# A hybrid encoder step with routed experts on one core: the order in which an expert's rows are laid over the 96 places of its block

## The chip, the cores and the metric

The kernel runs on one core of one Trainium2 chip. The metric is the device time of one execution in microseconds. The kernel before took 1379.6 us (median of three runs, 1379.13 to 1380.07).

## What is computed

One layer of a streaming encoder over 576 tokens (512 of a prompt, 64 of a sample), model width 1024. A first part (an input projection, a causal pooling mixer, gated linear attention, an output projection, a layer norm) gives `h`. Then comes a mixture of 32 experts, of which each token takes 4, and a second layer norm:

```python
def _moe(x2, w_router, b_router, w_gu, b_gu, w_down, b_down):
    logits = jnp.dot(x2, w_router) + b_router
    top_val, top_idx = lax.top_k(logits, TOP_K)          # 4 of 32
    gates = jax.nn.softmax(top_val, axis=-1)
    ...
    def block_fn(args):
        e, rows = args
        xb = x2[rows]
        gu = jnp.dot(xb, w_gu[e]) + b_gu[e]              # 1024 -> 2048
        gate, up = gu[:, :EXPERT_FF], gu[:, EXPERT_FF:]
        gate = jnp.minimum(gate, SWIGLU_LIMIT)
        up = jnp.clip(up, -SWIGLU_LIMIT, SWIGLU_LIMIT)
        hmid = gate * jax.nn.sigmoid(SWIGLU_ALPHA * gate) * (up + 1.0)
        return jnp.dot(hmid, w_down[e]) + b_down[e]      # 1024 -> 1024
    ...
    y = jax.ops.segment_sum(y_rows * sorted_gate[:, None], sorted_tok, num_segments=N)
```

576 tokens times 4 experts are 2304 rows, 72 for a mean expert. With the reference's own inputs its router gives the 32 experts 73, 75, 72, 70, 77, 61, 85, 76, 74, 61, 63, 82, 69, 75, 79, 75, 87, 65, 78, 69, 59, 52, 54, 92, 77, 71, 84, 73, 63, 80, 67 and 66 rows.

## The kernel before

All weights are float32 in HBM. An expert has four pieces of `w_gu` and two of `w_down`, 2 MB each. SyncE loads them (L423 to L441, `load` at L432) into a ring of eight slots, each piece 128 partitions of 16 KB, in the order of use. A piece is issued when the slot it goes to has been read: by VectorE's splits (`split_done`) for a slot that held `w_gu`, by TensorE's down product (`down_read`) for one that held `w_down`.

ScalarE turns each quarter of a piece of `w_gu` into a float16 high part (`hi`, L781), VectorE into a low part (`lo`, L1519), and TensorE multiplies with three float16 products (`unit`, through the helper at L853). The down product uses the float32 weights from the ring directly (`down`, again L853). Each expert is one block of at most `BLK` = 96 rows. The loop over the 32 experts `n` is written out, and each engine has the order of its work within an expert written by hand; TensorE takes `unit` 0 to 15, then `rows` (eight transposes of the gathered rows of expert n+1, L1097), then `down`.

The rows of a block are found like this. `rank` holds, for each token and expert, the token's place among the expert's rows (1 to the count, in token order) or 0. `onehot` (L1445) compares the rank of every token with the 96 numbers of `iota16` and gives a 0/1 matrix of tokens by places. `table` multiplies its transpose with a small table of token numbers and gates, so that partition p of the result holds the token whose rank is `iota16[p]`. `rows_of` (L1456 to L1464) makes two indices of it for each partition: the row of `h_rows` to read and the row of `part_rows` to write. For a place that no token has (a rank above the expert's count) both come out above the bound that the transfers are given, and such a row is not moved.

GpSimd issues for each expert one indirect gather of 96 rows of 4 KB, `xg` from `h_rows` (L581), and for 30 of the 32 experts one indirect scatter of 96 rows of 4 KB from `orow` to `part_rows` (L594). The gather for expert n+2 is issued once TensorE has transposed the rows of n+1; the scatter of n once ScalarE has weighed the result of `down` (`weigh`, L795). All these transfers and the weights' use the same 16 DMA engines.

In the kernel before, `iota16` is filled so that, with p = 6a + k (a from 0 to 15, k from 0 to 5), `iota16[p]` = 16k + a + 1. An expert with 72 rows then has places k = 0 to 3 filled for every a, k = 4 filled for a below 8, and k = 5 for none.

After the last expert SyncE loads `h_rows` and the four quarters of `part_rows` (L462), VectorE adds them (L1600), TensorE adds the last two experts, and the layer norm and the stores follow.

Of the kernel before, what the change touches and what calls it, by code (L numbers as in the profile page):

```python
# [53 lines left out]
BLK = 96  # L54
# [15 lines left out]
def build(nc, x_prompt, x_sample, state_pool, state_gla, w_in, w_pool, pool_scale, w_gate_up,  # L70
# [3 lines left out]
    with ExitStack() as ctx:  # L74
# [20 lines left out]
        def take(n, at=None):  # L95

            if at is None:
                at = cursor[0]
                cursor[0] += n
                assert cursor[0] <= 20408, cursor[0]  # L100
            return work[:, at:at + n]
# [5 lines left out]
        iota1 = take(P)  # L107
# [8 lines left out]
        iota16 = take(BLK // 2).bitcast(F16)  # L116
# [235 lines left out]
        def in_order(eng, s):  # L352


            n = [0]

            def step(ins):
                ins.then_inc(s, 1)
                n[0] += 1
                eng.wait_ge(s, n[0])  # L360
            return step
# [33 lines left out]
        def _(sp):  # L395
# [16 lines left out]
            for p, (_, c, s, _) in enumerate(PIECES):  # L412

                for dst, src, done in loads[:N_SMALL] if p == 2 else loads[N_SMALL:] if p == 3 else []:
                    sp.dma_start(dst, src).then_inc(done, 16)
                sp.dma_start(slot(s, 8, 512), w_in[0, :, c:c + 512].rearrange("(k p) n -> p k n", p=P))\
                  .then_inc(slot_in[s], 16)
# [795 lines left out]
        def _(dve):  # L1213
            step = in_order(dve, dve_order)
# [2 lines left out]
            step(dve.memset(info, 0.0))  # L1217
            step(dve.tensor_scalar(info[:, :, :, 3], small[:, 54:54 + TILES].unsqueeze(2).to_broadcast([P, TILES, E + 1]),
                                   float(PLACES), None, ALU.subtract))

            step(dve.tensor_copy(iota16.rearrange("p (a k) -> p a k", a=16),
                                 iota1[:, 0:BLK].rearrange("p (k a) -> p a k", a=16)))
            for t in range(TILES):
                n = ROWS[t]
                for b in range(2):
# [448 lines left out]
```

## Time and profile before

| | kernel before |
|---|---|
| median of three runs | 1379.6 us |
| time of the profiled execution | 1379.13 us |
| its span, first to last instruction | 1377.4 us |
| TensorE matmul busy | 1284.2 us, 93% |
| VectorE busy | 1008.3 us, 73% |
| ScalarE busy | 680.5 us, 49% |
| GpSimd busy | 121.9 us, 9% |
| bytes moved | 472.60 MB, 343 GB/s over the span |
| mean granted TensorE clock | 0.973 |

Times in a profile are counted from the start of the span. In the chain of work that ended last each step is followed back to what released it. A DMA's time to landing runs from its issue to the last of its parts. The share of a DMA queue is the time that its packets took, out of 16 engines times the stretch. With several requests queued on one engine the share of all engines is near 1 and can come out slightly above it.

### The profile page before, as it was taken

The page shows a single profiled execution, that of the slowest core. Times are in us where ns is not written, and L with a number is a line of the kernel's source. Part 1 is how long each engine was busy: PE and PEld are TensorE (multiplying, and loading weights), DVE is VectorE, ACT ScalarE, POOL GpSimd, SP SyncE. Part 2 cuts the span into 40 slices and gives each one's busy share as a digit, 9 for nine tenths or more (in the row PEclk, how much of TensorE's full clock was granted, in tenths as well). Part 3 has the DMA queues.
Part 4 walks back from the last instruction along what each step waited for, and adds up shares of the span by engine and source line. Part 5 has one row for each costly group of instructions (what it writes and reads, how often), then busy time and mean ns, then how long its engine had stood idle before and what let it go on. Part 6 is the DMA issues. An engine that isn't in the chain of part 4 may idle for free.

```text
span 1377.4 us, 34698 instructions
## 1 busy us (share of the span) xinstructions
PE 1284.2 (93%) x15188; PEld 881.0 (64%) x15188; DVE 1008.3 (73%) x1575; ACT 680.5 (49%) x814; POOL 121.9 (9%) x139
## 2 busy tenths in 40 slices
PE   6999999858999999999999999999999999999955
PEld 3446645446777776666677777776666676776722
DVE  4542436558888888888778888878887887888866
ACT  4431221145556556565556656556555665655511
POOL 1000811010000000000000000000000000000002
PEclk9999999959999999999999999999999999999987
DMA  9640154088999999999999999999999999999982
GB/s 319 225 170 1 64 190 207 23 314 315 403 410 414 409 412 411 412 403 406 411 408 410 406 412 413 408 415 414 414 398 410 408 411 411 414 413 412 406 350 71
DMA packets 50005, 472.60 MB, mean 343 GB/s; under 512 B 8541, under 2 KB 9332, under 8 KB 24636
## 3 DMA queue, kind: packets, MB, share of 16 engines
q1 hardware_dynamic: 38860, 436.22, 78.0%
q0 software_dynamic: 10336, 31.77, 6.5%
q8 instruction: 121, 1.98, 0.6%
q10 hardware_dynamic: 656, 2.36, 0.5%
q14 instruction: 32, 0.26, 0.0%
HBM read 446.43 MB, written 29.95 MB: 346 GB/s over the span
## 4 chain that ended last, share of the span: by engine, by line
PE 59%; DMA 12%; DVE 6%; issue 2%; ACT 1%; DVEq 0%; POOLq 0%
PE wide L853 43%; PE bank L853 15%; DMA ring<-in_w_gu 9%; DVE work L1519 3%; DMA work<-part_rows 2%; PE bank L1097 1%; DMA work<-h_rows,work 1%; ACT work L781 1%; DVE ring L1627 0%; DVE ring L1625 0%; DVE ring L1614 0%; DVE work L1445 0%; DVE work L1489 0%; DVE work L1492 0%; ACT work L786 0%
## 5 line engine op out<-in xcount | busy, mean ns | idle before, releaser
L1519 DVE SCALAR_TENSOR_TENSOR work<-ring,work 128x1024 f16<-128x1024 f32 x512 | 591.1, 1219 | 127.8 <-ACT work L781 127.7
L853 PE MATMUL wide<-ring,work 128*96 128x512 f32 (+4 forms) x1400 | 564.6, 562 | 1.5 <-ACT work L718 1.0
L781 ACT ACTIVATE work<-ring 128x1024 f16<-128x1024 f32 x512 | 503.8, 1050 | 76.1 <-DMA ring<-in_w_gu 69.4
L853 PEld LDWEIGHTS wide<-ring,work 128*96 128x96 f32 (+4 forms) x1400 | 214.4, 156 | 321.1 <-issue 297.0
L853 PE MATMUL wide<-work 128*128 128x96 f16 (+1 forms) x6262 | 302.5, 210 | 36.8 <-DMA work<-part_rows 17.4
L853 PEld LDWEIGHTS bank<-work 128*128 128x128 f16 (+4 forms) x6430 | 294.4, 101 | 33.4 <-issue 23.3
L853 PEld LDWEIGHTS wide<-work 128*128 128x128 f16 (+1 forms) x6262 | 278.0, 98 | 57.3 <-issue 22.6
L853 PE MATMUL bank<-work 128*128 128x96 f16 (+4 forms) x6430 | 298.5, 209 | 9.8 <-ACT work L754 3.8
L786 ACT ACTIVATE work<-work 128x384 f32<-128x384 f32 x64 | 33.5, 524 | 199.9 <-DVE work L1492 199.9
L795 ACT ACTIVATE work<-wide,work 96x1024 f32<-96x1024 f32 x30 | 33.2, 1106 | 119.3 <-PE wide L853 119.3
L581 POOL DMA_INDIRECT work<-h_rows,work x32 | 31.8, 995 | 504.9 <-PE bank L1097 475.8
L594 POOL DMA_INDIRECT part_rows<-work x30 | 28.1, 937 | 425.2 <-ACT work L795 425.2
L773 ACT ACTIVATE work<-bank 128x384 f16<-128x384 f32 x64 | 28.1, 488 | 44.9 <-PE bank L1097 44.8
L1494 DVE SCALAR_TENSOR_TENSOR work<-wide,work 128x384 f32<-128x384 f32 x32 | 17.8, 558 | 39.1 <-PE wide L853 39.1
L1097 PE MATMUL bank<-work 96*128 96x96 f32 x256 | 27.9, 253 | 14.0 <-DMA work<-h_rows,work 13.0
L1510 DVE SCALAR_TENSOR_TENSOR work<-bank,work 128x384 f16<-128x384 f32 x64 | 32.6, 550 | 10.5 <-ACT work L773 10.4
L853 PE MATMUL wide<-work,ring 128*128 128x512 f16 (+2 forms) x296 | 37.6, 285 | 0.0
L1504 DVE TENSOR_TENSOR work<-work 128x384 f32<-128x384 f32 x64 | 35.8, 560 | 2.2
L1501 DVE SCALAR_TENSOR_TENSOR work<-work 128x384 f32<-128x384 f32 x64 | 35.8, 559 | 2.2
L1408 DVE SCALAR_TENSOR_TENSOR ring<-ring,wide 128x1024 f32<-128x1024 f32 (+1 forms) x5 | 6.1, 1219 | 41.3 <-PE wide L853 41.3
L1237 DVE SCALAR_TENSOR_TENSOR ring<-ring 128x1024 f16<-128x1024 f32 x16 | 19.0, 1222 | 19.5 <-ACT ring L669 19.5
L1097 PEld LDWEIGHTS bank<-work 96*128 96x128 f32 x256 | 23.1, 144 | 14.2 <-DMA work<-h_rows,work 13.1
(190 smaller groups left out, 609.8 us busy)
## 6 DMA issues: line engine op xcount, KB each, us to landing
ring<-in_w_gu SPq DMA_DIRECT2D x128, 2048.0 KB, 23.9
ring<-in_w_down SPq DMA_DIRECT2D x64, 2048.0 KB, 28.1
part_rows<-work POOLq DMA_DIRECT2D x1, 10240.0 KB, 36.8
ring<-in_w_in SPq DMA_DIRECT2D x4, 2048.0 KB, 14.0
ring<-part_rows SPq DMA_DIRECT2D x3, 2560.0 KB, 28.5
ring<-in_w_out SPq DMA_DIRECT2D x2, 2048.0 KB, 9.5
h_rows<-work POOLq DMA_DIRECT2D x1, 2560.0 KB, 9.9
ring<-h_rows SPq DMA_DIRECT2D x1, 2560.0 KB, 22.3
```

The source lines that it names most:

```text
L581: pool.indirect_dma_start(xg, None, h_dram, bass.IndirectOffsetOnAxis(ap=tok_i[q], axis=0), bounds_check=PLACES - 1, oob_is_err=False)\
L594: pool.indirect_dma_start(part_dram, bass.IndirectOffsetOnAxis(ap=dst_i[p], axis=0), orow, None, bounds_check=TOPK * SPAN - 1, oob_is_err= ...
L773: act.activation(xhi[q][:, 4 * b:4 * b + 4, :], bank[b][:, 0:4 * BLK] .rearrange("p (k s) -> p k s", k=4), ACT.Copy, scale=X_UP).then_inc( ...
L781: act.activation(whi[u % BUFS], packed(s, u), ACT.Copy, scale=W_UP).then_inc(hi_done, 1)
L786: act.activation(sg, g1, ACT.Sigmoid, scale=SWISH).then_inc(sig_done, 1)
L795: act.activation(orow, wide[1 if isinstance(n, int) else 0][0:BLK, :], ACT.Copy, scale=slots[p][:, 5:6])\
L853: return pe.matmul(out, w, x, start=start, stop=stop, skip_group_check=True)
L1097: last = pe.transpose(bank[b][:, k * BLK:(k + 1) * BLK], xg[:, (4 * b + k) * P:(4 * b + k + 1) * P], ident[0:BLK, 0:BLK])
L1501: dve.scalar_tensor_tensor(u1, u1, 1.0, g1, ALU.add, ALU.mult).then_inc(gate_up, 1)
L1504: dve.tensor_tensor(hm[:, 4 * half:4 * half + 4, :], u1, sg, ALU.mult).then_inc(hm_done, 1)
L1510: dve.scalar_tensor_tensor(xlo[q][:, 4 * b:4 * b + 4, :], bank[b][:, 0:4 * BLK] .rearrange("p (k s) -> p k s", k=4), X_UP, xhi[q][:, 4 * b ...
L1519: dve.scalar_tensor_tensor(wlo[u % BUFS], packed(s, u), W_UP, whi[u % BUFS], ALU.mult, ALU.subtract).then_inc(split_done, 1)
```

## The change

One line of VectorE's preparation is changed. The 96 numbers of `iota16` are written as 1, 2, ..., 96 in place of the order above, so that partition p holds the token of rank p + 1. Everything downstream follows `iota16`: the same tokens go through the same expert, each on another partition of the block, and the unfilled places are the last partitions of the block.

```diff
@@ VectorE, preparation
             step(dve.tensor_scalar(info[:, :, :, 3], small[:, 54:54 + TILES].unsqueeze(2).to_broadcast([P, TILES, E + 1]),
                                    float(PLACES), None, ALU.subtract))
-
-            step(dve.tensor_copy(iota16.rearrange("p (a k) -> p a k", a=16),
-                                 iota1[:, 0:BLK].rearrange("p (k a) -> p a k", a=16)))
+            step(dve.tensor_copy(iota16, iota1[:, 0:BLK]))
             for t in range(TILES):
```

## Rows read from the trace of the kernel before

**Rows 1.** The page: busy shares, then TensorE's clock and DMA in 40 slices.

```profile
PE 1284.2 (93%) x15188; PEld 881.0 (64%) x15188; DVE 1008.3 (73%) x1575; ACT 680.5 (49%) x814; POOL 121.9 (9%) x139
...
PEclk9999999959999999999999999999999999999987
DMA  9640154088999999999999999999999999999982
```

**Rows 2.** Two stretches of the experts: length, busy time by engine, clock, DMA, GB/s.

```profile
324.00:1025.00 701.00, 690.26 (x9453) 497.42 (x9451) 578.08 (x891) 411.15 (x467) 42.45 (x45) 1.00 1.00 407
1025.00:1282.00 257.00, 250.66 (x3423) 179.90 (x3422) 208.59 (x314) 147.71 (x167) 15.19 (x16) 1.00 1.01 411
```

**Rows 3.** Chain of work that ended last: start, length, what; transposes of four experts.

```profile
324.20 0.68 PE bank L1097 x8
324.88 13.75 PE wide L853 x32
...
403.06 8.43 PE bank L853 x197
411.50 8.27 PE wide L853 x192
...
1024.02 0.68 PE bank L1097 x8
...
1281.85 0.68 PE bank L1097 x8
```

**Rows 4.** Waits in 600 to 1000, then in 1025 to 1290: total, times, longest.

```profile
ACT work L781 <- DMA ring<-in_w_gu: 4.2, 4, 1.6
...
ACT work L781 <- DMA ring<-in_w_gu: 63.2, 25, 5.4
```

**Rows 5.** The weights' issues (L432) of four experts, and their times to landing.

```profile
L432 SPq DMA_DIRECT2D ring<-in_w_gu x4: 328/380/437, 459.0 to 466.7; - x4
DMA to landing us min/median/max: 12.7/17.7/22.6
...
L432 SPq DMA_DIRECT2D ring<-in_w_gu x4: 328/379/431, 714.4 to 722.1; - x4
DMA to landing us min/median/max: 17.4/23.2/28.4
...
L432 SPq DMA_DIRECT2D ring<-in_w_gu x4: 328/380/432, 1031.6 to 1039.3; - x4
DMA to landing us min/median/max: 28.4/33.5/37.4
...
L432 SPq DMA_DIRECT2D ring<-in_w_gu x4: 328/328/432, 1224.7 to 1235.6; - x4
DMA to landing us min/median/max: 29.8/33.5/35.8
```

**Rows 6.** DMA queues and row transfers from 600 to 900: packets, MB, share; issues.

```profile
q1 hardware_dynamic: 8000, 116.49, 94.5%
q0 software_dynamic: 2126, 5.77, 5.5%
q8 instruction: 33, 0.54, 0.7%
...
work<-h_rows,work POOLq DMA_INDIRECT x10, 10.7
part_rows<-work POOLq DMA_INDIRECT x9, 10.1
```

**Rows 7.** Who waited for the gathers (L581), in the whole span.

```profile
  PE bank L1097: 13.0, 1
...
DMA to landing us min/median/max: 4.5/10.7/11.9
```

**Rows 8.** Timeline of VectorE at the changed line.

```profile
7.76 0.24 DVE L1221 CAST work<-work 128x96 f16<-128x96 f32 x1
10.63 0.69 DVE L1227 SCALAR_TENSOR_TENSOR work<-bank,work 128x512 f16<-128x512 f32 x1 [1.30 <-ACT work L676]
```

**Rows 9.** The end of the same chain of work.

```profile
1305.02 8.45 PE wide L853 x192
1313.48 31.97 DMA work<-part_rows
1345.50 9.28 PE wide L853 x20
```

## The prediction

> **What bounds the kernel now.** I read the page first. TensorE is busy 93% of the span, and the digits of its clock are 9 in nearly every slice, so it runs at its upper level, 2.4 GHz; but the DMA digits are 9 from the thirteenth slice to the last but one as well [rows 1]. Two resources are full at once in the experts, and the change touches only one of them, DMA. So the question is which of the two sets the pace, and from when.
>
> The stretches say that it changes hands. From 324 us to 1025 us TensorE is busy 690.26 of 701 us, from 1025 to 1282 us 250.66 of 257; the DMA engines' share is 1.00 and 1.01 [rows 2]. In the chain of work the transposes of expert rows come at 324.20, at 1024.02 (22 experts later) and at 1281.85 (8 more): 31.81 us an expert first, 32.23 after [rows 3]. TensorE's own work in an expert is 13.75 + 8.43 + 8.27 + 0.68 = 31.13 us [rows 3]. So in the first stretch the pace is nearly TensorE's; in the second something holds it by 1.1 us.
>
> The waits name it. ScalarE, the first to read a piece of weights, waits 4.2 us for pieces of `w_gu` between 600 and 1000 us, but 63.2 us in 25 waits between 1025 and 1290 [rows 4]. The reason stands in the time from issue to landing: its longest in an expert is 22.6 us at 459, 28.4 at 714, 37.4 at 1031, and 35.8 at 1224 [rows 5]. A piece has landed when the last of its 16 parts has. Between the first and the third of these lie 18 experts, so the last part falls behind its issue by (37.4 - 22.6) / 18 = 0.8 us an expert. The ring hides this until its eight slots are used up, near 1025 us; then the lag can't grow, and the last DMA engine sets the pace.
>
> The same comes out of what an expert asks of a DMA engine. Between 600 and 900 us the weights' queue took 94.5% of 16 x 300 us for 116.49 MB, 38.9 us a MB, so a 16 KB packet takes 0.638 us; an expert has 6 x 128 of them, 48 an engine, 30.6 us. The rows' queue took 5.5% for 5.77 MB, 45.8 us a MB, 0.187 us for a row of 4 KB [rows 6]. 5.77 MB are 1409 rows in 19 transfers, 74 each: places that no token has move no bytes. A mean expert moves 72 rows in and 72 out, 9 an engine, 1.7 us. Fetching instructions adds 0.7% of 31.8, 0.2 us [rows 6]. Sum 32.5 us for the mean engine, against 31.8 at which TensorE asks. DMA is short by 0.7 us an expert, as the landing times say.
>
> **The change, part by part.** The copy at L1221 takes 0.24 us now, and nearby VectorE waits 1.30 us for ScalarE [rows 8]. With plain operands it takes between 0 and 0.24 us, so between -0.24 and 0; I take 0, being far ahead of the experts.
>
> The instructions of every engine stay as they are in number and size, and so do the bytes. What moves is which partition holds which row, and with it which DMA engine carries it. No row of the profile tells engines apart. I take it that the 96 partitions of an indirect transfer go to the 16 engines in order, six to each; the other reading is a rival below. For 72 rows eight engines now have 5 and eight have 4. After the change twelve have 6 and four have none. Summed over the 32 counts of the router: now 158 rows for the first engine, falling evenly to 127 for the last, 4.9 to 4.0 an expert. After it 192 for each of the first eight (6.0), then 190, 179, 157, 124, 75, 31, 10 and 2.
>
> The first ten engines go from a mean of 4.70 rows to 5.95, 1.25 more, and each row is carried twice, in and out: 2.5 packets an expert. A packet's price is 0.187 us by the rows' own queue, and 0.159 us if 4 KB go at the weights' rate of 38.9 us a MB [rows 6]. That is 0.40 to 0.47 us an expert. From about the fourth expert the landing lag only grows, so an engine that is behind has always something queued, and what it carries more delays its end one for one, whether the ring still hides it or not. Over 28 experts: 11.1 to 13.1 us. For single engines, the smallest among the ten is the first (192 - 158 = 34 rows, 1.06 an expert, 9.5 to 11.1 us), the largest the eighth (47 rows, 1.47 an expert, 13 to 15.4 us). The eleventh has 16 rows more, 5 us; the last five have fewer.
>
> In the first stretch it costs nothing at once: TensorE stays at 31.8 us. The lag grows by 0.8 + 0.45 = 1.25 us an expert in place of 0.8; from 22.6 us at the seventh expert it reaches 37 after 12 experts instead of 18, near 830 to 860 us. From there the pace should be some 32.7 us an expert in place of 32.2. What is late next is ScalarE's high part, then VectorE's low part, then TensorE's unit. The gathers land in 10.7 us and have a whole expert to do so; TensorE waited for one just once [rows 7]. A sixth row adds below 1 us behind queued packets and nobody waits.
>
> At the end the rows of `part_rows` come in at full rate, in whole transfers, and the chain has 31.97 us of them from 1313.48 [rows 9]. They queue behind the weights on the same engines, so the shift at the last weights is the shift at the end. Sum against the profiled execution: 1379.13 + 11 = 1390.1. Its own time is 0.5 us under the median of the three runs, so 1390.6 there. Of 11.1 to 13.1 I take 11, the lower end, because the engine that is last now need not be one of the ten.
>
> The Trainium skill bears on this in "DMA: Bandwidth & Descriptors", section "Latency and other measured facts": engines 7 and 15 are usually slower than the others, with a guessed cause. No row here names an engine. If only the last one were slow, the change would take rows from it (the faster rival below); if the eighth is as slow, it gets 6.0 rows for 4.6, and the largest term above, 13 to 15.4 us, holds.
>
> **The rivals.**
>
> *The engines share one bound.* If the pace is set by the total rate (407, then 411 GB/s [rows 2]) and not by each engine, rows moved from one engine to another cost nothing as long as all are kept busy: 1379.6 us. For it: the rate is the same in both stretches. Against it: all 16 shares are full while landing falls behind, which each engine's own limit explains as well, and a last engine that carries more must still end later. The same time comes out if the change doesn't do what it says to the engines: if partition p goes to engine p mod 16, both orders are even.
>
> *The slow engines are the ones relieved: faster.* If the parts that land last belong to the last four or five engines, they lose 3 or more rows an expert (4.2 to 0.9), 3.3 x 2 x 0.187 = 1.2 us, more than the 0.8 us by which they fall behind. Then TensorE keeps 31.81 us, which saves 8 x (32.23 - 31.81) = 3.4 us before 1282 us, and the end, whose transfers no longer queue behind so long a lag (37 us against 22), gains perhaps 3 more: 1373 us. It decides only if the first eleven engines are all ahead of these by more than the 0.45 us an expert that they gain. The landing times give the last of 16 parts alone [rows 5] and speak neither for nor against; but the mean engine by the sums above is already short by 0.7 us, so most engines must be near the limit, and that speaks against.
>
> *TensorE hides it.* If the lag of the second stretch were a matter of order in the ring and not of rate, TensorE would set the time and the change would be within 2 us. Against it: 63.2 us of waits for weights [rows 4].
>
> **How the numbers follow.** The forecast (each engine has its own limit, an engine of the first eleven is last) has 0.76; the shared bound or another spread of the partitions 0.14; relief of the slow engines 0.07; TensorE hiding it 0.03. The forecast's own range is 5 to 15.4 us, 1384.6 to 1395.0. The whole range reaches down to 1381 for cases in which the last engine of now is relieved and the next is near, and to 1396: 1381 to 1396. A measurement of this kernel tells 0.2%, 2.8 us, from nothing. Part of the forecast's case could fall within that, so slower by more 0.75, within 0.17, faster 0.08.
>
> **What would show it.** Right: instruction counts, bytes and the first stretch's 31.8 us an expert as before; landing times that grow by about 1.25 us an expert from 459 us on and stop near 37; ScalarE's waits for `w_gu` beginning near 850 us and summing to well over 63 us; then some 32.7 us an expert; a rate below 411 GB/s in that stretch; the chain's piece of `part_rows` still near 32 us. Wrong: landing times like those of now (shared bound or even spread); landing times that stay under 30 us to the end (relief); the growth of the lag without a longer pace (TensorE hides it). If the packets are dearer beside each other than apart, the step would be right and the term too small.

## The result, and the profile after

The changed kernel took 1396.39 us (median of four runs, 1395.68 to 1398.9) beside 1379.84 us for the kernel before in the same runs. The ratio is 1.012, with a 95% interval of 1.0103 to 1.0139: 16.5 us slower, where 11 were forecast and 1396 was the upper end of the range. The profiled execution, a fifth one, took 1402.07 us, span 1400.3, so it lies 5.7 us over the median and 22.9 us over the profiled execution of the kernel before. 4.3 us of that difference were there before the first expert, where the change does nothing: the first transposes stand at 299.66 us here and at 295.35 us before.

The page of the kernel after: busy shares, and TensorE's clock and DMA in 40 slices.

```profile
PE 1294.9 (92%) x15188; PEld 887.9 (63%) x15188; DVE 1010.5 (72%) x1575; ACT 678.1 (48%) x814; POOL 122.2 (9%) x139
...
PEclk9999999959999999999999999999999999999987
DMA  9540154087999999999999999999999999999972
```

Instruction counts are those of [rows 1], and so are the bytes, 472.60 MB. Two stretches of the kernel after: length, busy time by engine, clock, DMA share, GB/s.

```profile
324.00:850.00 526.00, 514.60 (x6938) 369.11 (x6939) 428.53 (x667) 300.43 (x345) 32.12 (x34) 0.99 0.99 399
850.00:1300.00 450.00, 430.46 (x5849) 311.14 (x5848) 358.79 (x540) 255.08 (x289) 25.73 (x27) 0.99 1.00 403
```

The rate in the late stretch is 403 GB/s where [rows 2] has 411, and TensorE stands idle for 4.3% of it, where it stood for 2.5%. The weights' issues (L432) of four experts and their times to landing:

```profile
L432 SPq DMA_DIRECT2D ring<-in_w_gu x4: 327/380/438, 466.0 to 473.7; - x4
DMA to landing us min/median/max: 14.5/19.8/24.9
...
L432 SPq DMA_DIRECT2D ring<-in_w_gu x4: 328/379/431, 592.9 to 600.6; - x4
DMA to landing us min/median/max: 20.9/28.1/32.4
...
L432 SPq DMA_DIRECT2D ring<-in_w_gu x4: 327/379/432, 721.3 to 729.0; - x4
DMA to landing us min/median/max: 25.5/31.9/37.2
...
L432 SPq DMA_DIRECT2D ring<-in_w_gu x4: 327/328/432, 849.4 to 861.4; - x4
DMA to landing us min/median/max: 31.1/35.9/37.2
```

The longest time to landing grows from 24.9 to 37.2 us in the eight experts between 466 and 721 us, 1.5 us an expert against 0.8 before [rows 5], and then stops at the same 37 us: the ring is used up near 720 us in place of 1025. The chain of work of the kernel after, at some experts and at the end:

```profile
299.66 1.56 PE bank L1097 x8
...
396.05 13.73 PE wide L853 x32
...
618.09 13.73 PE wide L853 x32
...
759.45 30.05 DMA ring<-in_w_gu
...
876.77 1.31 PE bank L1097 x8
...
1305.93 0.68 PE bank L1097 x8
...
1337.61 31.96 DMA work<-part_rows
```

Between 396.05 and 618.09 lie seven experts, 31.7 us each, as before. Between 876.77 and 1305.93 lie 13, 33.0 us each, where the late stretch before had 32.2 [rows 3]. The chain runs over a load of `w_gu` from 759 us on, so from there the weights' transfers hold the work. ScalarE's waits for weights in 850 to 1300 us:

```profile
ACT work L781 <- DMA ring<-in_w_gu: 105.4, 42, 5.5
```

The last load of `part_rows` takes 31.96 us in the chain, as in [rows 9]. The shape is what was forecast: same pace, faster growing lag, full ring earlier, longer pace from there. Only the size is larger.

### The profile page after: what moved, and what is told of

Same layout as the page of the kernel before. It is cut to its first block, busy times and chain, and to the rows that moved or that the text cites. A ratio compares the mean times of both kernels' runs of the same rounds, so it can differ in the third digit from the quotient of the medians.

```text
span 1400.3 us, 34698 instructions
## 1 busy us (share of the span) xinstructions
PE 1294.9 (92%) x15188; PEld 887.9 (63%) x15188; DVE 1010.5 (72%) x1575; ACT 678.1 (48%) x814; POOL 122.2 (9%) x139
## 2 busy tenths in 40 slices
DMA packets 50005, 472.60 MB, mean 337 GB/s; under 512 B 8541, under 2 KB 9332, under 8 KB 24636
## 4 chain that ended last, share of the span: by engine, by line
PE 48%; DMA 19%; DVE 8%; ACT 3%; issue 3%; DVEq 0%; POOLq 0%
PE wide L853 36%; DMA ring<-in_w_gu 16%; PE bank L853 11%; DVE work L1517 4%; ACT work L781 3%; DMA work<-part_rows 2%; PE bank L1097 1%; DMA work<-h_rows,work 1%; DVE ring L1625 0%; DVE ring L1623 0%; DVE work L1443 0%; DVE ring L1612 0%; DVE work L1487 0%; ACT work L786 0%; DVE work L1490 0%
## 5 line engine op out<-in xcount | busy, mean ns | idle before, releaser
L853 PE MATMUL wide<-work 128*128 128x96 f16 (+1 forms) x6262 | 308.1, 211 | 49.5 <-DVE work L1517 22.8
L853 PEld LDWEIGHTS wide<-work 128*128 128x128 f16 (+1 forms) x6262 | 283.2, 100 | 70.4 <-DVE work L1517 26.0
L581 POOL DMA_INDIRECT work<-h_rows,work x32 | 31.9, 998 | 506.7 <-PE bank L1097 478.1
L1406 DVE SCALAR_TENSOR_TENSOR ring<-ring,wide 128x1024 f32<-128x1024 f32 (+1 forms) x5 | 6.1, 1220 | 43.0 <-PE wide L853 43.0
L1317 DVE SCALAR_TENSOR_TENSOR ring<-ring,work,bank 64x128 f32<-64x128 f32 x32 | 8.9, 335 | 32.9 <-PE bank L853 32.7
## 6 DMA issues: line engine op xcount, KB each, us to landing
ring<-in_w_in SPq DMA_DIRECT2D x4, 2048.0 KB, 13.3
```

Of the source, the lines that this page charges most:

```text
L581: pool.indirect_dma_start(xg, None, h_dram, bass.IndirectOffsetOnAxis(ap=tok_i[q], axis=0), bounds_check=PLACES - 1, oob_is_err=False)\
L853: return pe.matmul(out, w, x, start=start, stop=stop, skip_group_check=True)
```

## The experiments

Engines are numbered here by runs of six partitions: engine a serves partitions 6a to 6a + 5. Row packets are rows of 4 KB, gathered or scattered, counted over all 62 transfers from the router's counts. The cuts of the edits leave out the line that each replaces. Engine 0 carries 306 in the kernel before and 372 after, the eighth (engine 7) 282 and 372.

**Token order or load?** Two kernels separate what the change couples: neighbouring tokens next to each other, and full and empty engines.

```diff
+            places = iota16.rearrange("p (a k) -> p a k", a=16)
+            step(dve.tensor_copy(places[:, :, 0:4], iota1[:, 0:64].rearrange("p (a k) -> p a k", a=16)))
+            step(dve.tensor_copy(places[:, :, 4:6], iota1[:, 64:BLK].rearrange("p (k a) -> p a k", a=16)))
```

> Places are filled so that neighbouring ranks (1 to 4, 5 to 8, ...) lie on neighbouring partitions as after the change, but each run of six partitions gets 4 or 5 rows, as before it. Theory A (what costs is the load of the fullest DMA engines, six partitions an engine): 1380 us, as before, between 1377 and 1383. Rival B (what costs is the token order itself: neighbouring tokens' rows read and written next to each other in HBM): 1393 to 1397 us, as after the change.

```diff
+            step(dve.tensor_copy(iota16[:, 0:72].rearrange("p (a k) -> p a k", a=12),
+                                 iota1[:, 0:72].rearrange("p (k a) -> p a k", a=12)))
+            step(dve.tensor_copy(iota16[:, 72:BLK], iota1[:, 72:BLK]))
```

> Engines 0 to 11 get six rows each for 72 rows and 12 to 15 only what is above 72, as after the change, but each engine's rows are 12 ranks apart, as far apart as before. For counts below 72 the loads are evener than after the change (five or six each). Theory A: 1393 to 1397 us. Rival B: 1380 us.

The first took 1382.98 us beside 1380.48 for the kernel before (ratio 1.0012, 1.0000 to 1.0024), the second 1393.42 (1.0102, 1.0087 to 1.0116). So the load of the engines carries most of the time. Neighbourhood costs 0 to 3.3 us by the first interval. The second kernel's fullest engine carries 366 packets and not 372, which may be why it costs 3.6 us less than the change; no run separates that from neighbourhood.

**Which engines are full.** The order of the change, begun at another partition (here 48; the other kernel 72):

```diff
+            step(dve.tensor_copy(iota16[:, 48:BLK], iota1[:, 0:48]))
+            step(dve.tensor_copy(iota16[:, 0:48], iota1[:, 48:BLK]))
```

> Order of the change, but rank 1 on partition 48: full engines are 8 to 15 and 0 to 3, those with none are 4 to 7. Theory A: slower than before too, 1385 to 1402 us, and not the same as after the change: engines 11 to 15 get 1.6 to 2 rows an expert more than before, so if the engines that are last are among them, near 1400 us; if they are among 4 to 7, near 1385 us. Rival C (every order that fills twelve engines and empties four costs the same, whichever they are): 1396 us.

> Order of the change with rank 1 on partition 72: full engines are 12 to 15 and 0 to 7, those with few or none are 8 to 11. Theory A: 1385 to 1402 us, by the base pace of the engines that are full; the lowest of the three starts (0, 8, 12) relieves the engines that are last today. Rival C: 1396 us.

Start 8 took 1395.32 us (1.0113, 1.0099 to 1.0128), start 12 took 1392.07 (1.0090, 1.0075 to 1.0104). All three starts are slower by 11.6 to 16.5 us. Whichever of the three sets of four engines is relieved (12 to 15, 4 to 7 or 8 to 11), most of the others are full, and the time is longer. No run relieves engines 0 to 3. The differences are a few microseconds.

Start 12 fills engine 15 and relieves 8 to 11, and it is the cheapest; start 8 leaves engine 7 two gathered rows of 145 and is still 14.8 us slower than the kernel before. The Trainium skill says in "DMA: Bandwidth & Descriptors", section "Latency and other measured facts", that engines 7 and 15 are usually slower than the others. If its numbers are those of the runs of six partitions, this is not what decides here. The packet records of the kernel before show no slow engine in the quiet part of an expert either: of the weights' packets that start 12 to 30 us after a gather's issue, 98% take 611 to 624 ns, and one slow engine of 16 would hold 6% of them.

**A smaller dose.**

```diff
+            places = iota16.rearrange("p (a k) -> p a k", a=16)
+            step(dve.tensor_copy(places[:, :, 0:5], iota1[:, 0:80].rearrange("p (a k) -> p a k", a=16)))
+            step(dve.tensor_copy(places[:, :, 5:6], iota1[:, 80:BLK].rearrange("p (k a) -> p a k", a=16)))
```

> A smaller dose of the same: the first fifteen runs of six partitions get five rows in rank order and one run gets what is over, so that over all transfers the first eleven engines carry 14 to 36 row packets more than before (after the change 28 to 90 more). Theory A with 0.187 us a packet and an engine near the eighth (30 more) as the last one: 1379.8 + 5.6, so 1385.5 us, between 1383 and 1388. Theory A' (only a sixth row on an engine is dear, five are free): 1380 us.

1387.84 us beside 1381.05 (1.0050, 1.0036 to 1.0063), 6.8 us more. A smaller dose costs less, though not in proportion: engine 7 has 30 packets more and pays 6.8 us, 0.23 us a packet; in the change it has 90 more for 16.5, 0.18. This alone doesn't tell a dearer packet from another last engine: at 0.187 us a packet engine 7 would pay 5.6 us here and 16.8 us in the change.

**Scatters and gathers apart.** The scatters are replaced by their semaphore's increment, in both orders:

```diff
-                pool.indirect_dma_start(part_dram, bass.IndirectOffsetOnAxis(ap=dst_i[p], axis=0),
-                                        orow, None, bounds_check=TOPK * SPAN - 1,
-                                        oob_is_err=False).then_inc(scattered, 16)
+                pool.sem_inc(scattered, 16)
```

> The kernel before without the 30 scatters: their results never reach memory, so the rows of the first 30 experts are missing from the output. An engine then carries 4.5 packets an expert less, 0.84 us, and asks for 31.7 us an expert, as much as TensorE (31.8). Theory A: no landing lag grows, TensorE's pace to the end, 1368 to 1375 us. Rival D (the pace is TensorE's and ScalarE's order and not DMA): 1379 to 1380 us.

> The changed kernel without the 30 scatters, same rows missing from the output. A full engine carries six packets an expert in place of twelve, and asks for about 32.0 us: the lag grows by about 0.2 us an expert, 6 us in all, which the ring hides. Theory A: within 2 us of the same kernel with the old order, where the full kernels lie 16.5 us apart. Rival E (the order costs something in itself, through gathers or the block, whatever the load): 8 us or more apart.

1360.57 us (0.9855, 0.9838 to 0.9871) and 1374.20 us (0.9952, 0.9936 to 0.9967). Both expectations missed, and the second is the telling one: 13.6 us between the two orders with half of the row packets gone. In neither order does the time to landing reach the 37 us of a full ring: near 1220 us the times to landing are 23.7 us at most in the first kernel and 34.5 us in the second. The chain at the end shows where the lag comes out all the same; first the old order without scatters, its weights at 1222 us and then its chain:

```profile
L432 SPq DMA_DIRECT2D ring<-in_w_gu x4: 327/380/440, 1221.7 to 1229.4; - x4
DMA to landing us min/median/max: 13.9/18.4/23.7
...
1308.64 19.12 DMA work<-part_rows
```

The new order without scatters, the same:

```profile
L432 SPq DMA_DIRECT2D ring<-in_w_gu x4: 327/380/439, 1225.4 to 1233.1; - x4
DMA to landing us min/median/max: 24.2/30.1/34.5
...
1312.50 28.76 DMA work<-part_rows
```

The last load of `part_rows` takes 19.12 us with a short lag in front of it and 28.76 us with a long one. It queues behind the weights on every engine. So the ring hides a lag from the experts' pace, not from the end; my expectation for the second kernel had forgotten this, though the prediction had it. In the kernels with scatters this piece is 31.97 and 31.96 us; their times to landing had stopped growing near 36 to 37 us, so the lag in front of it was about the same in both.

13.6 us for the gathers' rows alone are much: engine 7, with the most added, gathers 192 rows in place of 145, so if an engine's own rows were all of it, a gathered row would cost 13.6 / 47 = 0.29 us or more. Its packet takes 0.196 us in these two kernels, so something else is lost with it. The same pair without the gathers:

```diff
-                pool.indirect_dma_start(xg, None, h_dram,
-                                        bass.IndirectOffsetOnAxis(ap=tok_i[q], axis=0),
-                                        bounds_check=PLACES - 1, oob_is_err=False)\
-                    .then_inc(gathered[q2], 16)
+                pool.sem_inc(gathered[q2], 16)
```

> The kernel before without the 32 gathers: every expert works on the zeros that the block was cleared to, so the experts' part of the output is not the reference's; the scatters stay. Theory G, formed from the runs so far (during a gather the weights' packets of all engines take about 0.82 us in place of 0.62, during a scatter they don't): an engine's demand falls from 32.5 us to 48 x 0.616 + 4.5 x 0.162 + 0.2 = 30.5 us an expert, below TensorE's 31.8, no landing lag grows, 1355 to 1361 us. Theory A with 0.187 us for every row packet alike: as without the scatters, 1360.6 us, with a lag that still grows a little.

> The changed kernel without the 32 gathers, same part left out. Theory G: a full engine asks for 48 x 0.616 + 6 x 0.162 + 0.2 = 30.7 us, still under TensorE's pace, so no lag grows in either order and the two lie within 2 us, where without the scatters they lay 13.6 us apart. Theory A: the same 13.6 us apart, since 5 of 10 packets go in both cases.

1362.60 us (0.9841, 0.9813 to 0.9868) and 1361.73 us (0.9850, 0.9825 to 0.9874): no difference between the orders. The weights' time to landing stays put, here the new order without gathers, at 459 and 1222 us:

```profile
L432 SPq DMA_DIRECT2D ring<-in_w_gu x4: 328/380/432, 459.2 to 484.9; - x4
DMA to landing us min/median/max: 10.3/15.2/20.7
...
L432 SPq DMA_DIRECT2D ring<-in_w_gu x4: 328/379/431, 1221.6 to 1229.4; - x4
DMA to landing us min/median/max: 11.3/16.2/20.5
```

Without gathers DMA keeps up with TensorE in either order, so this pair bounds nothing on a scatter's row. But taken out of the changed kernel the gathers free 34.7 us and the scatters 22.2. These two differences go across sets of runs in which the kernel before took 1379.84, 1381.75 and 1381.05 us, so they are good to about 2 us.

**Is it the indirect form?**

```diff
-                pool.indirect_dma_start(xg, None, h_dram,
-                                        bass.IndirectOffsetOnAxis(ap=tok_i[q], axis=0),
-                                        bounds_check=PLACES - 1, oob_is_err=False)\
-                    .then_inc(gathered[q2], 16)
+                pool.dma_start(xg, h_dram[0:BLK, :]).then_inc(gathered[q2], 16)
```

> The kernel before with each gather replaced by a plain transfer of the first 96 rows of h_rows from the same queue, so that the experts work on the wrong rows and every engine brings in 6 rows. It tells whether the slow weights' packets come with the indirect form. If they come with any 4 KB rows read from HBM into 96 partitions: weights' packets of 0.8 us for 5 us, and 1388 to 1397 us, as every engine is as full for reads as the twelve are after the change. If they come with the indirect form alone: packets stay at 0.62 us, and the time is 1372 to 1378 us.

1393.76 us (1.0087, 1.0066 to 1.0107), 12.0 us more than the kernel before. A plain transfer of 96 rows slows the stream as well, so the indirect form isn't needed for it. It moves a third more bytes than the gather (96 rows for 72) and loads every engine with six rows, so its price isn't that of the form alone. The rate around one gather shows how. The kernel before, a gather issued at 453.0 us and a scatter issued at 467.9 us (columns as above; the last is GB/s):

```profile
449.00:453.00 4.00, 3.60 (x56) 2.92 (x53) 2.26 (x5) 1.69 (x4) 0.03 (x1) 1.00 1.00 426
457.00:459.00 2.00, 2.00 (x6) 0.82 (x5) 2.00 (x2) 2.00 (x3) 0.00 (x0) 1.00 1.04 340
459.00:461.00 2.00, 2.00 (x6) 0.67 (x5) 2.00 (x3) 1.98 (x3) 0.00 (x0) 1.00 1.00 305
461.00:463.00 2.00, 2.00 (x6) 0.80 (x5) 2.00 (x3) 1.29 (x2) 0.00 (x0) 1.00 0.97 356
463.00:465.00 2.00, 2.00 (x6) 0.81 (x5) 1.41 (x6) 0.00 (x0) 0.00 (x0) 1.00 1.02 434
472.00:474.00 2.00, 2.00 (x52) 2.00 (x49) 2.00 (x3) 1.08 (x2) 0.00 (x0) 1.00 0.96 408
474.00:476.00 2.00, 2.00 (x48) 1.97 (x46) 1.97 (x4) 0.13 (x1) 0.00 (x0) 1.00 1.01 428
```

The kernel with the plain transfer, issued at 453.1 us:

```profile
456.00:458.00 2.00, 2.00 (x6) 0.68 (x5) 2.00 (x3) 2.00 (x3) 0.00 (x0) 1.00 0.93 346
458.00:460.00 2.00, 2.00 (x6) 0.78 (x5) 2.00 (x3) 2.00 (x3) 0.00 (x0) 1.00 1.02 334
460.00:462.00 2.00, 2.00 (x6) 0.81 (x5) 2.00 (x3) 1.98 (x3) 0.00 (x0) 1.00 1.03 319
```

The engines are all busy in every one of these windows, but while a gather's rows come in they move 305 to 356 GB/s, all rows included, in place of 426 to 434; while a scatter's go out, 408 to 428. The gather takes about 6 us of this, at some 100 GB/s less: 0.6 MB not moved, 1.3 to 1.4 us for each engine, on top of the rows' own 0.3 MB, 0.7 us. That is about 2.0 us for 4.5 rows, an estimate of 0.4 us a row in this one gather.

**The even orders.** The old order begun at partition 72 (shown) and at partition 24, to find the last engine and perhaps spare it:

```diff
+            places = iota16.rearrange("p (a k) -> p a k", a=16)
+            ranks = iota1[:, 0:BLK].rearrange("p (k a) -> p a k", a=16)
+            step(dve.tensor_copy(places[:, 12:16, :], ranks[:, 0:4, :]))
+            step(dve.tensor_copy(places[:, 0:12, :], ranks[:, 4:16, :]))
```

> The even order of before with its first run of six on partition 72: engines 12 to 15 carry 44 to 54 row packets more over all transfers, engines 0 to 11 carry 10 to 22 fewer. From the two starts measured so far engines 12 to 15 are not the last ones (full, they cost 11.6 us at most, so at 306 packets they are no worse than the last engine of before). Theory A: 0.7 to 3 us under the kernel before, 1377 to 1379.5 us. Rival F (all engines alike but for their rows): 1380 us, since the fullest engine has 306 packets either way.

> The even order of before with its first run of six on partition 24: engines 4 to 7 carry 304 packets in place of 286, engines 8 to 13 carry 286 in place of 273, engines 0 to 3 carry 50 fewer. If the engine that was last in both kernels is one of 4 to 11 (start 12, which spares all of them and two more starts, cost 11.6 us and start 0 cost 16.5): 2 to 4 us over before, 1382 to 1384 us. If it is among 0 to 3: 1378 us.

1382.68 us (1.0012, 1.0000 to 1.0024) and 1382.05 us (1.0007, 0.9993 to 1.0022). In the first the gain of 0.7 to 3 us didn't come, and rival F, no difference, fits. The second is 0.3 us over its own kernel before (1381.75), neither 2 to 4 us over it nor under it. Neither points to one last engine, and no order tried beats the kernel before.

Put side by side, the time goes with the fullest engine. Where it carries 306 packets (the neighbouring tokens and the two even orders) the cost is 0.3 to 2.5 us, with 320 it is 6.8, with 366 12.9, and with 372 (the three starts) 11.6 to 16.5 us. It is not a straight line, and the same 372 packets cost different amounts.

## Why the prediction was right or wrong

- *Two resources full at once, DMA behind by 0.7 us an expert, the ring hiding it until 1025 us.* Right. Without the scatters or without the gathers the kernel before gains 20.5 and 19.2 us.
- *The change moves rows between engines and nothing else; six partitions an engine.* Right as to bytes, counts and which engines carry the rows: with even loads and the new neighbourhood the cost is 0 to 3.3 us, with the uneven loads and the old spacing 12.9 us.
- *Hidden or not, the extra load delays the end one for one, since the last loads queue behind the weights.* Right, and shown by the pair without scatters: near 1222 us its times to landing differ by 10.8 us, and its last loads of `part_rows` by 9.6.
- *The lag grows by 1.25 us an expert, is full near 830 to 860 us, then 32.7 us an expert.* Right in kind, short in size: 1.5 us, full near 720 us, 33.0 us.
- *2.5 packets an expert at 0.159 to 0.187 us, over 28 experts 11.1 to 13.1 us, of which the lower end.* This is the step that failed: the price of a row packet. It took every row packet for as dear as its own time on its own engine, and put at nothing what a gather's rows take from the weights' packets beside them. The own time was about right: in the packet records of the kernel before a gathered row takes 202 ns and a scattered one 162. At these, 1.25 rows more each way over 28 experts are 12.7 us, an estimate near the upper end of the term. What was left out can be read in the same records. I add up what the weights' packets that start 3 to 12.5 us after a gather's issue take above 616 ns (those over 1.1 us left out), for the 26 gathers between 400 and 1250 us. It comes to 0.94 us an engine and gather before and 1.10 after, each within 0.03 (standard error), so 4.5 us over 28 experts. Together this estimate is 17 us, where 16.5 were measured. The pair without scatters gives 0.91 and 1.13 us, 6.4 us over 28 experts, and 6.9 for the gathered rows themselves: 13.3 us, where 13.6 were measured. The profile before held the hint: a row's own duration says nothing on what the weights' packets beside it lose, and the rate in a gather's window does. I also rounded to the lower end because the last engine could be one of those relieved; the starts 0, 8 and 12, all slower by 11.6 us or more, show no gain for any of these three sets of four engines.
- *The rivals.* A shared bound or an even spread of the partitions would have given 1380 us for all starts. Yet one part of the cost is shared: the slowing beside a gather falls on all engines and lasts longer when some engines have six rows. Relief of the slow engines didn't occur at any of three starts. TensorE doesn't hide it: it stands idle for 4.3% of the late stretch in place of 2.5%.

What stays open: which engine is last in either kernel, as the two even orders that should have told it moved by no more than the measurement can tell; how exactly the cost divides between a longer slowing beside the gather and a fuller engine, as the split above is an estimate from one profile a kernel and no run changes one without the other; and why rows that come in slow the weights while rows that go out don't.

## What to carry to other kernels

When a stream keeps the DMA engines full, the places that are left empty in a gather's block are work that some engines don't have: spread them over all sixteen, since here the time rose with the fullest engine's rows. A ring of buffers hides an engine's lag from the loop, and the first transfers after the loop pay for it. Price a transfer that is mixed into a stream by the rate of its window, not by its own packets' durations.

## What the runs showed of the hardware

In the packet records of the kernel before, between 400 and 1250 us, a 16 KB packet of the weights takes by the time since the last gather's issue (mean, ns):

```
us since issue   0-1  1-2  2-3  3-4  4-5  5-6  6-7  7-8  8-9  9-10 10-11
gather           617  616  616  621  771  838  837  790  717  641  622
scatter          617  616  618  618  616  613  613  613  615  614  616
```

A gather's rows lengthen the weights' packets beside them from 616 to 838 ns; a scatter's rows, of the same size and number, leave them as they are. With the changed order the stretch holds about 1 us longer (742 ns at 9 to 10 us), and a gather's row packets start within 5.6 us of each other in place of 4.7. Of the packets of weights that start 5 to 7 us after a gather's issue (785 before, 869 after) none takes under 700 ns, also after the change, where four engines have almost no rows: the slowing is common to all engines.

The records don't name engines, but almost always 16 packets are under way, and on each engine the next starts within a few ns of the last one's end. So they can be joined into 16 strands; two whose packets end at nearly the same time may get swapped. Over 25 gathers, 3 to 13 us after the issue, 291 of 400 strands of the kernel before hold 4 or 5 gathered rows. With the changed order 189 hold six and 62 none or one. This is the spread that the prediction assumed. In the kernel after, the weights' packets that start 5 to 7 us after the issue take 813 ns on average in the strands with none or one row, and 814 ns in those with five or more.
